# High and low tokens as one 512-column operand in the products that are added to the stream, with two VectorE additions

## The reference

```python
def first_block(x, ...):                 # two layers
    x = x + conformer_conv(rmsnorm(x, ..), ...)      # ends in u @ w_pw2 + b_pw2
    x = x + swiglu(rmsnorm(x, ..), ...)              # (silu(h @ wg) * (h @ wu)) @ wd, 2816 hidden channels
    x = x + dilated_attention(rmsnorm(x, ..), ...)   # ends in o @ w_o, 768 -> 1024
    x = x + swiglu(...)
    return rmsnorm(x, final_norm)

def second_block(x, c, ...):             # two layers
    # sh, sc, g: six vectors for each layer, of silu(c) @ ada_w + ada_b
    h = _rms_norm(x, ..) * (1.0 + sc1) + sh1
    x = x + g1 * (mixer(h) @ w_out)      # even mixer, then odd mixer
    h = _rms_norm(x, ..) * (1.0 + sc2) + sh2
    x = x + g2 * swiglu(h)
```

## Time and profile before

| | us |
|---|---|
| three runs | 1307.89, 1310.67, 1311.06 (median 1310.67) |
| the profiled execution, its own time | 1311.96 |
| its span, first to last instruction | 1310.6 |
| TensorE matmul busy | 1210.4 (92%) |
| VectorE busy | 960.3 (73%) |
| ScalarE busy | 653.4 (50%) |
| GpSimd busy | 108.7 (8%) |
| mean granted TensorE clock | 0.971 |

### The profile page before, as it was taken

The page is one execution under the profiler, slowest core; times in us unless marked ns, Lnnn a source line. Parts: engine busy times, 40 slices in busy tenths (PEclk is TensorE's granted clock), DMA queues, the critical chain, the costliest instruction groups (busy, mean ns, idle before and its releaser), DMA issues.

```text
span 1310.6 us, 24770 instructions
## 1 busy us (share of the span) xinstructions
PE 1210.4 (92%) x9796; PEld 1152.6 (88%) x9796; DVE 960.3 (73%) x1853; ACT 653.4 (50%) x1142; POOL 108.7 (8%) x106
## 2 busy tenths in 40 slices
PE   4978899999998999999978788999989879999999
PEld 4957899999987999999967678999989767999999
DVE  5966598878776888878886658888875555766653
ACT  5326554445446544445555664544444765545431
POOL 2001100002000200004000112000011112100000
PEclk9999899999999999999998989999999989999999
DMA  7487688877853678787633325887865422555552
GB/s 275 142 210 92 225 301 261 252 265 265 271 179 123 196 262 263 236 276 249 219 110 103 103 91 177 272 255 252 275 230 184 133 89 83 191 179 186 184 193 65
DMA packets 81126, 259.36 MB, mean 198 GB/s; under 512 B 8904, under 2 KB 20424, under 8 KB 81012
## 3 DMA queue, kind: packets, MB, share of 16 engines
q1 hardware_dynamic: 81012, 257.79, 62.1%
HBM read 252.68 MB, written 5.08 MB: 197 GB/s over the span
## 4 chain that ended last, share of the span: by engine, by line
PE 68%; DVE 18%; ACT 6%; issue 4%; DMA 1%; POOL 1%; DVEq 0%; ACTq 0%
PE ps L521 61%; DVE wlo L1188 6%; DVE aacc L1194 2%; DVE CV L1194 1%; PE ps L582 1%; DVE X L1194 1%; DMA raw<-wall 1%; ACT HH L840 1%; ACT oS L840 1%; PE ps L617 1%; ACT eS L840 1%; PE ps L613 1%; PE ps L612 1%; PE ps L621 1%; DVE tn L1191 1%
## 5 line engine op out<-in xcount | busy, mean ns | idle before, releaser
L521 PE MATMUL ps<-HH,whi 128*128 128x256 f32 (+1 forms) x2152 | 625.7, 291 | 32.9 <-DVE wlo L1188 13.9
L521 PE MATMUL ps<-HH,wlo 128*128 128x256 f32 (+1 forms) x2152 | 615.3, 286 | 0.0
L521 PE MATMUL ps<-HL,whi 128*128 128x256 f32 (+1 forms) x2152 | 615.0, 286 | 0.0
L840 ACT ACTIVATE whi<-raw 128x1024 fp32r<-128x1024 f32 x363 | 381.0, 1056 | 333.3 <-PE ps L521 328.0
L1188 DVE TENSOR_TENSOR wlo<-raw,whi 128x1024 fp32r<-128x1024 f32 x363 | 444.2, 1228 | 37.2 <-ACT whi L840 36.7
L521 PEld LDWEIGHTS ps<-HH,whi 128*128 128x128 f32 x2152 | 415.7, 193 | 51.7 <-issue 22.4
L521 PEld LDWEIGHTS ps<-HL,whi 128*128 128x128 f32 x2152 | 415.6, 193 | 0.4
L521 PEld LDWEIGHTS ps<-HH,wlo 128*128 128x128 f32 x2152 | 415.4, 193 | 0.0
L521 PE MATMUL ps<-GH,whi 128*128 128x256 f32 x704 | 198.2, 282 | 0.6 <-DVE bcol L1414 0.5
L521 PE MATMUL ps<-GL,whi 128*128 128x256 f32 x704 | 197.5, 281 | 0.0
L521 PE MATMUL ps<-GH,wlo 128*128 128x256 f32 x704 | 197.5, 280 | 0.0
(11 more groups left out here) (207 smaller groups left out, 984.7 us busy)
## 6 DMA issues: line engine op xcount, KB each, us to landing
raw<-wall SPq DMA_DIRECT2D x363, 512.0 KB, 4.3
araw<-ada SPq DMA_DIRECT2D x96, 512.0 KB, 4.7
UR<-uscr SPq DMA_DIRECT2D x24, 142.0 KB, 3.3
scratch<-bvec SPq DMA_DIRECT2D x1, 3072.0 KB
oBB<-kbias SPq DMA_DIRECT2D x16, 192.0 KB, 2.5
aTB<-scratch SPq DMA_DIRECT2D x12, 128.0 KB, 2.4
X<-x_in SPq DMA_DIRECT2D x2, 512.0 KB, 5.9
out<-X SPq DMA_DIRECT2D x8, 128.0 KB, 3.1
```

The source lines that it names most:

```text
L521: ins = pe.e.matmul(o, l, r, start=(kt == p.order[0] and i == 0), stop=(kt == p.order[-1] and i == 2))
L840: ac.then_inc(ac.e.activation(o, i, func, **kw), sem)
```

## The change

In the added products a step is two matmuls: whi with the high and the low tokens side by side, 512 columns, and wlo with the high tokens, 256 columns. The bank then holds two results of 256 columns, and `residual` adds both to `X`, the second half first. For this the high and low tiles lie next to each other in memory (`H2`, `G2`), so the tokens of all products change their addresses. In the last step of a tile the two matmuls are swapped.

```diff
-        HH = [sb(f"HH{i}", [P, KD, T + 2], F32R) for i in range(2)]
-        HL = [sb(f"HL{i}", [P, KD, T + 2], F32R) for i in range(2)]
+        H2 = [sb(f"H{i}", [P, KD, 2, T + 2], F32R) for i in range(2)]
+        HH, HL = [h[:, :, 0, :] for h in H2], [h[:, :, 1, :] for h in H2]
...
-            GH, GL = sb("GH", [P, KF, T], F32R, st), sb("GL", [P, KF, T], F32R, st)
+            G2 = sb("G", [P, KF, 2, T], F32R, st)
+            GH, GL = G2[:, :, 0, :], G2[:, :, 1, :]
...
+                        elif both is not None:
+                            mm = [(ps[:, 0:2 * T].rearrange("p (a b) -> p a b", a=2), wh, both[:, kt, :, 0:T]),
+                                  (ps[:, 0:T], wl, hh[:, kt, 0:T])]
+                            if kt == p.order[-1]:
+                                mm.reverse()
...
                 product(f"dn{f}", GH, GL, T, lambda kt: pe.wait_ge(S.gl, KF * f + kt + 1),
-                        lambda nt: sums(f"dn{f}", nt))
+                        lambda nt: sums(f"dn{f}", nt), both=G2)
...
+                    if op == ALU.mult:
+                        stt(X[:, nt, :], ps[:, T:2 * T], scale(nt), X[:, nt, :], op, ALU.add, S.xl)
+                    else:
+                        tt(X[:, nt, :], ps[:, T:2 * T], X[:, nt, :], ALU.add, S.xl)
+                    dv.settle()
                     stt(X[:, nt, :], ps[:, 0:T], scale(nt), X[:, nt, :], op, ALU.add, S.ev)
```

More of the change, by code:

```diff
@@ L340, in __init__ @@
         self.hi, self.lo, self.mm, self.ev = new("hi"), new("lo"), new("mm"), new("ev")
-        self.xg, self.hh, self.hlv, self.hlp = new("xg"), new("hh"), new("hlv"), new("hlp")
+        self.xl, self.xg, self.hh, self.hlv, self.hlp = new("xl"), new("xg"), new("hh"), new("hlv"), new("hlp")
         self.sq, self.sqa, self.tot = new("sq"), new("sqa"), new("tot")
@@ L493, in tensor_program, with product @@
             pe = Queue(nc.tensor)
-            def product(name, hh, hl, width, ready, after=None, before=None, middle=None):
+            def product(name, hh, hl, width, ready, after=None, before=None, middle=None, both=None):
                 p = PROD[name]
@@ L515, in product @@
                             o, cols = ps[:, 0:2 * P], slice(tt * P, (tt + 1) * P)
-                            mm = [(hh[:, kt, cols], wh), (hh[:, kt, cols], wl), (hl[:, kt, cols], wh)]
+                            mm = [(o, hh[:, kt, cols], wh), (o, hh[:, kt, cols], wl), (o, hl[:, kt, cols], wh)]
+                        elif both is not None:
[3 more added lines that the diff above has]
+                                mm.reverse()
                         else:
                             o = ps[:, 0:width]
-                            mm = [(wh, hh[:, kt, 0:width]), (wh, hl[:, kt, 0:width]), (wl, hh[:, kt, 0:width])]
-                        for i, (l, r) in enumerate(mm):
+                            mm = [(o, wh, hh[:, kt, 0:width]), (o, wh, hl[:, kt, 0:width]), (o, wl, hh[:, kt, 0:width])]
+                        for i, (o, l, r) in enumerate(mm):
                             ins = pe.e.matmul(o, l, r, start=(kt == p.order[0] and i == 0),
-                                              stop=(kt == p.order[-1] and i == 2))
+                                              stop=(kt == p.order[-1] and i == len(mm) - 1))
                         if last or kt == p.order[-1]:
@@ L596, in convolution @@
                 pe.then_inc(ins, S.lnt)
-                product("pw2", HH[LN_SET], HL[LN_SET], T, lambda kt: pe.wait_ge(S.lnl, kt + 1))
+                product("pw2", HH[LN_SET], HL[LN_SET], T, lambda kt: pe.wait_ge(S.lnl, kt + 1),
+                        both=H2[LN_SET])
             def feed_forward(f):
@@ L672, in dilated @@
                 product("outd", HH[YD_SET], HL[YD_SET], T,
-                        lambda kt: pe.wait_ge(S.dhl, 3 * (2 * (kt % 2) + 1) + kt // 2 + 1), None, before)
+                        lambda kt: pe.wait_ge(S.dhl, 3 * (2 * (kt % 2) + 1) + kt // 2 + 1), None, before, both=H2[YD_SET])
             def project(tiles, s):
@@ L782, in even @@
                 product("mixe", HH[NORM_SET[4]], HL[NORM_SET[4]], T + 2, norm_ready(4), **slotted(slot))
-                product("oute", HH[YE_SET], HL[YE_SET], T, ready, None, lambda kt: slot(46 + PROD["oute"].order.index(kt)))
+                product("oute", HH[YE_SET], HL[YE_SET], T, ready, None, lambda kt: slot(46 + PROD["oute"].order.index(kt)),
+                        both=H2[YE_SET])
             def odd():
@@ L821, in odd @@
                 product("mixo", HH[NORM_SET[6]], HL[NORM_SET[6]], T + 2, norm_ready(6), **slotted(slot))
-                product("outo", HH[YO_SET], HL[YO_SET], T, lambda kt: pe.wait_ge(S.ohl, kt + 1), None, lambda kt: slot(24 + kt))
+                product("outo", HH[YO_SET], HL[YO_SET], T, lambda kt: pe.wait_ge(S.ohl, kt + 1), None, lambda kt: slot(24 + kt),
+                        both=H2[YO_SET])
             convolution()
```

## The result

The changed kernel took 1331.14 us (median of 4, 1330.05 to 1333.36) beside 1310.74 us for the kernel before (4 runs on the same chip, 1307.89 to 1311.06). The ratio is 1.0163, with a 95% interval of 1.0143 to 1.0182: slower by 20.4 us by the medians, 21 by the ratio. 1325.7 was forecast, with 1317 to 1335 as the range. The profiled execution took 1333.36 us, 2.2 above its median; its span is 1332.1.

What follows compares the result with a forecast made beforehand. TensorE's product matmuls were taken to bound the kernel, VectorE's chain the ends of the short products. Short products +12.3, dn products -0.3 and clock +3.0 made +15.0 us, so 1325.7 us, range 1317 to 1335.

Steps and rivals of the forecast that it cites:

- What bounds the short products: In pw2, outd, oute and outo, VectorE's chain of additions, gains, low parts and wlo units sets the end.
- Rival 4: VectorE's delay is taken up before the products' ends, so the 12.3 us go: 1310 to 1312 us; chance 0.05.
- The price of a tile: Each added VectorE instruction takes 478 or 417 ns; with settling, 0.51 us a tile in the second block, 0.45 in the first.
- The short products, +12.3: Added instructions lengthen oute and outo by 4.1 us each, outd by 2.7, pw2 by 1.4; together +12.3 us.
- pw2's part, +1.4: In pw2, VectorE's wait at tile 4 hides five additions, and the three left cost 1.4 us.
- What a step saves, 15 ns: Each of 944 TensorE steps loses one matmul and weight load, saving 15 ns, halfway between 10.7 and 19.
- The row that I had called no proof: Plain fp32 sum on TensorE, 216 to 218 ns an instruction, suggesting 19 ns saved a step; reads tokens at half rate.
- the -2.1 forecast: In dn3, 176 steps by 15 ns give -2.6 us and the last addition +0.5.
- The dn products, -0.3: dn0 -0.4, dn1 +1.6, dn2 +0.6 and dn3 -2.1 us: additions eat most of the matmul saving of 10.6.
- the earlier first addition that was to give 1.0 back: In dn1, 66 steps saving 15 ns each bring the first addition 1.0 us earlier; dn1 in all +1.6.
- The clock, +3.0: Longer TensorE waits at the starts of gu1 and gu3 lower its clock behind them, 1.5 us each.
- Rival 5: New token addresses quicken all gu and mix matmuls, 116 ns for 119.5, -20 us: about 1305 us; chance 0.03.

Runs made afterwards that it cites:

- e2: Changed kernel, but each step is three 256-column matmuls into two results, and VectorE still adds both: 1333.05 us, ratio 1.0161.
- e13: Changed kernel with GpSimd working on only 4 of 256 columns in oute, result incomplete: 1328.25 us, one run.
- e12: Kernel before with GpSimd working on only 4 of 256 columns in oute, result incomplete: 1308.07 us, one run.
- e7: Changed kernel with the change kept only in pw2, outd, oute and outo; new layout everywhere, dn products with three matmuls and one addition: 1322.99 us.
- e1: Changed kernel reduced to its layout: tiles side by side, but three matmuls into one result and one addition, as before: 1306.82 us, ratio 0.996.
- e3: Changed kernel with its two matmuls a step, but VectorE adds only the bank's first half, so the result is incomplete: 1305.6 us, ratio 0.9938.
- e5: Changed kernel with matmuls of unused results filling TensorE's waits: 1318.03 us, ratio 1.006.
- e6: Kernel before with matmuls of unused results filling its own, shorter TensorE waits: 1307.14 us, ratio 0.9959.

## Why the prediction was right in sign and short in size

**What bounds the short products: right.** VectorE's chain sets their ends. The time of outd, oute and outo grew with its instructions, and e2, without the long matmul, has the same stretches to 0.02 us. Rival 4, a delay that is taken up, is out.

**The price of a tile: right.** 484 and 424 ns measured for 478 and 417, and e13 less e12 gives 3.64 us over seven tiles, 0.52 each for 0.51.

**The short products, +12.3: right over e1, wrong over the kernel before.** e7 over e1 is +16.2 with the clock, for 15.3. In the two full traces, though, it is some 7.6. The step that failed is the layout, which the sum had at nothing. In oute and outo nothing was idle to hide the additions, as forecast, but part of what was busy was no work: the gain in the earlier trace rows stands there with 0.91 us, and the same form takes 0.35 elsewhere. Those 0.56 us were a collision, which e1, with the tiles side by side and no addition more, no longer has. By it oute is 1.21 us shorter and outo 1.69, and only the rest of oute's 1.4 came with the additions. pw2's part, +1.4, can't be read from a pair of profiles (+1.2 in e7, -0.7 in the full change); the means of nine with one addition and five with two are 1.7 us apart.

**What a step saves, 15 ns: wrong, 5.** The bounds were 0, 10.7 and 19, and the value taken was the middle of the upper two. It is 5 ns from the base that the forecast had (352 to 347), and 9 where the three matmuls ran at their other pace (356, e1 and e3), in both cases below the 10.7 that go with the instruction. In order of time, dn3's last steps (start, mean length):

```profile
1319.61 0.39 PE L530 MATMUL ps<-G,whi 128*128 128x512 f32 x1
1319.84 0.28 PE L530 MATMUL ps<-G,wlo 128*128 128x256 f32 x1
1319.96 0.39 PE L530 MATMUL ps<-G,whi 128*128 128x512 f32 x1
1320.18 0.28 PE L530 MATMUL ps<-G,wlo 128*128 128x256 f32 x1
1320.30 0.39 PE L530 MATMUL ps<-G,whi 128*128 128x512 f32 x1
```

From the start of a 512 to the next matmul it is 0.22 to 0.23 us, from a 256 0.12: some 230 and 117 ns. The long one has about 17 ns over the 213.3 of its columns, where the plain fp32 sum has 2 to 4. The row that I had called no proof was none. dn3 gave -0.5 us from first to last addition, and its matmuls 0.9 over the whole product, for the -2.1 forecast with its addition.

The Trainium skill (TensorE: Matmul & The Clock Gate, "Back-to-back issue gap") would have 216 and 109 ns. These are its numbers for a matmul by itself. Trace and page differ by 14 and 8 ns, and the measurement decides for this stream: with a fresh weight load beside each fp32r matmul the gap is far above 2.5 ns.

**The dn products, -0.3: wrong, +5.5 over e1.** Of this, 704 steps that save 10 ns less than forecast make up to 7 us, but not all of it counts. dn1 is the largest miss. Its additions cost their full price (+3.0 us of 3.15), and the earlier first addition that was to give 1.0 back gave nearly nothing at 5 ns a step. That made TensorE wait 4.13 us at mixe, where it had waited 0.16, and the low clock came on top. The prediction followed dn1's end to its number and did not ask what starts there.

**The clock, +3.0: wrong, some 8.7 (e5 and e6).** The step that failed is that the wait grows and the clock falls once behind it, at gu1 and gu3 only. The waits came in two at gu1, gu2 and gu3, with a few matmuls between (4.0, 5.3 and 3.8 us in all, where some 3.7, over 6 and 6 were expected), and new ones of 1.5 and 4.1 us appeared at mixd and mixe. From the shifts just ahead of and behind the slow stretches in the full trace, gu1 has 2.7 us, mixe 2.4, gu3 1.3, dn2 1.1, gu0 0.6 and gu2 0.5. gu2 and dn2, which I had left at their old cost because they were slow already, were slow for longer.

**The addresses.** Rival 5 was looked for in the gu and mix products, where the pace stayed (gu0 -0.3 us, gu1 +0.6, gu3 -0.8; the same in every profile with this layout). The layout did matter, by way of VectorE's and GpSimd's turns in the short products: e1 is 4.7 us faster than before, 2.9 of it in oute and outo. The sign was the rival's, the mechanism none of mine. The prediction's reason for the rival, that gu0 and gu1 differ by 1.6 ns a matmul for their buffers' places alone, is shown by no run; new places moved them by 0.3 and 0.8.

**The sum.** 12.3 - 0.3 + 3.0 was forecast; with waits filled the kernels are 10.9 apart for 12.0, and the clock adds 8.7 for 3.0. The first agreement is partly luck: less in the short products (GpSimd's collisions gone) stands against more in dn. So is part of the total: over the layout alone the change costs 24 us and more for the 15.0, and the layout's own 4.7, which the sum did not have, brought it back to 20.4. What stays open is what chooses between the two paces of a dn product, why GpSimd's subtraction is slower with the tiles side by side, whether anything appears only when short and dn products are changed together, and some 2 us of the profiled run ahead of pw2, which other runs don't have.

## What to carry to other kernels

Before an instruction is added to a chain that sets an engine's end, compare each duration in it with the same form elsewhere in the trace: one that is 2.6 times the usual may be a collision that goes or comes when something shifts by 0.1 us, so the layout alone should be run as a case of its own. A longer TensorE wait can cost more than its length, since the matmuls behind it may run at the lower clock; count each place where one appears, those behind a stage that merely ends later too, and try to fill it with matmuls whose result nobody uses. A merge of two matmuls saved 5 to 9 ns a step here, so it pays only where the second result costs nothing on another engine's chain. And before a few tenths of a microsecond are put down to an edit, look whether kernels without it have both values.

## What the runs showed of the hardware that I had not expected

- Matmuls with unused results in TensorE's waits made the changed kernel 13 us (1%) faster and the kernel before 4.4 us, at a granted clock of 1.00 where it had been 0.50.
- An fp32r matmul of 512 columns with its weight load takes some 230 ns from start to start, 17 over its columns; one of 256 columns 117, 10 over.
- dn0's 528 matmuls take 61.97 or 62.67 us (352 or 356 ns a step), with nothing between, and either value appears with either place of the tokens (before 61.98, e6 62.67; e7 61.97, e1 62.67). With 352 matmuls it was 61.09 in e3, and no second value appeared.
- The place of the tokens does go with a small, repeated change of pace in the gu products: gu1 88.21 us before and in e6, 88.8 in all kernels with H side by side; gu3 118.82 and 117.99.
- GpSimd's subtraction of 128 by 256 takes 0.75 us with the high and low tiles apart and 0.84 with them side by side.
- In oute and outo a gain on VectorE takes 0.92 us where it starts 0.04 us ahead of a GpSimd instruction and 0.35 where it starts 0.14 ahead; with GpSimd on 4 columns it is 0.35 always in oute, which is 2.2 us shorter.
